# The gated MLP of a hybrid decoder block: convolving the up units where the matmuls left them, in PSUM

## The reference

```python
h = rms_norm(x, g_pre_ffn) * (1.0 + sc2) + sh2
u = h @ w_up                                   # 1024 -> 2 * 2816
u = causal_depthwise_conv(u, conv_w) + conv_b  # width 3, per channel
gate, val = split(u, 2)
y = (gelu(gate) * val) @ w_down                # 2816 -> 1024
x = x + gt2 * rms_norm(y, g_post_ffn)
```

## Time and profile before

| | |
|---|---|
| median of 3 runs | 2221.29 us (2219.47 to 2221.75) |
| the profiled execution | 2221.01 us, of which the span 2218.9 us |
| PE busy | 2169.8 us, 98% of the span |
| DVE, ACT, POOL busy | 1414.3 us (64%), 780.1 us (35%), 313.3 us (14%) |
| mean clock granted to TensorE | 0.995 of full speed |
| ACT copies out of the banks, line 1724 | 176 of 595 ns |
| DVE, lines 2239, 2241, 2242 | 176 each of 646, 955 and 1044 ns on average |

### The profile page before, as it was taken

One profiled execution on the slowest core, in us unless ns is written; L12 is line 12 of the kernel. 1 busy time (PEld: TensorE's weight loads), 2 busy tenths in 40 slices (PEclk: granted clock), 3 DMA queues, 4 the chain that ended last, 5 costly groups with the idle time before them and its releaser, 6 DMA issues.

```text
span 2218.9 us, 32623 instructions
## 1 busy us (share of the span) xinstructions
PE 2169.8 (98%) x12955; PEld 1747.8 (79%) x12955; DVE 1414.3 (64%) x2386; ACT 780.1 (35%) x1537; POOL 313.3 (14%) x182
## 2 busy tenths in 40 slices
PE   6999999999999989999999999999999999999998
PEld 4776788888887768888888778888888877888886
DVE  3577677775866576787565757466565575566654
ACT  3555543334355342222334633211143444211112
POOL 2322354444300013323000000000000000000000
PEclk9999999999999999999999999999999999999999
DMA  9965687787663456767755254666746444666663
GB/s 367 399 239 195 251 292 257 280 303 280 241 257 116 171 190 261 264 259 269 302 200 207 98 209 171 256 257 264 297 158 249 151 147 160 262 247 234 236 244 121
DMA packets 123551, 519.27 MB, mean 234 GB/s; under 512 B 8831, under 2 KB 39817, under 8 KB 74249
## 3 DMA queue, kind: packets, MB, share of 16 engines
q1 hardware_dynamic: 123401, 517.19, 62.8%
HBM read 401.81 MB, written 115.34 MB: 233 GB/s over the span
## 4 chain that ended last, share of the span: by engine, by line
PE 87%; DVE 5%; ACT 3%; issue 2%; DMA 2%; SPq 0%; POOL 0%; DVEq 0%; ACTq 0%; POOLq 0%
PE ps L820 18%; PE ps L822 18%; PE ps L821 18%; PE ps L842 4%; PE ps L844 4%; PE ps L843 4%; PE ps L1279 3%; PE ps L1281 3%; PE ps L1280 3%; PE ps L1255 1%; PE ps L1254 1%; PE ps L1253 1%; PE ps L919 1%; PE ps L966 1%; PE ps L767 1%
## 5 line engine op out<-in xcount | busy, mean ns | idle before, releaser
L820 PE MATMUL ps<-hTh,wt 128*128 128x512 f32 x1416 | 559.7, 395 | 2.2 <-DVE hTl L1876 2.0
L821 PE MATMUL ps<-hTl,wt 128*128 128x512 f32 x1416 | 552.3, 390 | 0.0
L822 PE MATMUL ps<-hTh,wt 128*128 128x512 f32 x1416 | 552.3, 390 | 0.0
L1724 ACT ACTIVATE ub<-ps 128x512 f32<-128x512 f32 x176 | 104.7, 595 | 654.9 <-PE ps L822 642.4
L820 PEld LDWEIGHTS ps<-hTh,wt 128*128 128x128 f32 x1416 | 266.3, 188 | 64.3 <-issue 8.8
L822 PEld LDWEIGHTS ps<-hTh,wt 128*128 128x128 f32 x1416 | 266.4, 188 | 56.2
L821 PEld LDWEIGHTS ps<-hTl,wt 128*128 128x128 f32 x1416 | 266.6, 188 | 53.3
L2239 DVE TENSOR_SCALAR cv<-ub,CW 128x512 f32<-128x512 f32 x176 | 113.7, 646 | 281.6 <-ACT ub L1724 279.3
L721 POOL TENSOR_TENSOR wt<-raw,wt 128x1024 fp32r<-128x1024 f32 x72 | 176.4, 2455 | 318.5 <-ACT wt L1362 311.5
L2242 DVE SCALAR_TENSOR_TENSOR cv<-ub,CW,cv 128x512 f32<-128x512 f32 x176 | 183.8, 1044 | 6.2
L820 PE MATMUL ps<-hTh,wt_more 128*128 128x512 f32 x472 | 186.3, 395 | 0.1
(11 more groups left out here) (350 smaller groups left out, 3492.4 us busy)
## 6 DMA issues: line engine op xcount, KB each, us to landing
wt<-split_w SPq DMA_DIRECT2D x192, 1024.0 KB, 4.9
split_w<-wt SPq DMA_DIRECT2D x92, 1024.0 KB, 7.1
wt_more<-split_w SPq DMA_DIRECT2D x92, 1024.0 KB, 4.9
raw<-in_w_up_dram SPq DMA_DIRECT2D x22, 1024.0 KB, 9.3
XN<-in_w_down_dram SPq DMA_DIRECT2D x32, 512.0 KB, 9.4
XT<-in_w_ada_dram SPq DMA_DIRECT2D x10, 1024.0 KB, 12.0
XN<-in_x_dram SPq DMA_DIRECT2D x4, 2048.0 KB, 11.0
raw<-in_w_in_dram SPq DMA_DIRECT2D x8, 1024.0 KB, 14.9
```

The lines of the kernel that those rows point to most:

```text
L820: mm(ps[:, bank, :], w, hTh[:, k, :], start=(k == 0), stop=False)
L821: mm(ps[:, bank, :], w, hTl[:, k, :], start=False, stop=False)
L822: ins = mm(ps[:, bank, :], wl(slot)[:, k, :], hTh[:, k, :], start=False, stop=(k == KD - 1))
L1724: act.activation(ub[:, u, 2:], ps[:, u, :], ACT.Copy).then_inc(s["acc_taken"], 1)
```

## The change

The copy into `ub` goes. `take_up(u)` reads bank u three times with a scale and a bias: the last tap and the bias for columns 2 to 511, and for columns 0 and 1 the same with a bias that already holds what the two tokens of the last block add. These biases (`EG`) are made by DVE at the start of each block's up stage in six small operations. DVE's `conv(u)` reads the bank for the two other taps, then keeps two columns of it, and only then counts `acc_taken`. The gelu is written back to bank u, the product of gate and value to bank 2 + u (`ps[:, 2 + u]`), and the high and low parts and the four sums are made from there. In blocks 1 to 3, outside the last group, the first half of product 0 goes to `P32` in an operation of its own, and the sums wait for ACT's first copy (`ph_ready`).

PE's waits move with it: units 0 and 1 of a step wait for products 0 and 1 of the step before (`prod_ready`), units 2 and 3 for its last low part (`p_ready`), and the first four tiles of `last_down` for the two products and the last low part of the last step (`first_half`). DVE's wait for the old `conv_done` of a buffer goes, and ACT's `take_up` waits instead for the product of the step before that read the same half of `cv`.

```diff
...
@@ -357,9 +357,10 @@
         Y = fb("Y", [P, TT, D])
-        ub = fb("ub", [P, 4, 2 + BT])
+        EG = fb("EG", [P, 3, 2 * NFF])
+        fb("EG_rest", [P, 4 * (2 + BT) - 6 * NFF])
         cv = fb("cv", [P, 4, BT])
-        P32 = fb("P32", [P, 8, 256])
+        P32 = fb("P32", [P, 5, 256])
         ffn.close()
...
@@ -1192,6 +1195,16 @@
+                def bank_free(at, u):
+                    if at < 4:
+                        pe.wait_ge(s["acc_taken"], eb_ + E_IN)
+                    elif u < 2:
+                        pe.wait_ge(s["prod_ready"], b * (2 * STEPS) + at // 4 * 2 - 1 + u)
+                    else:
+                        pe.wait_ge(s["p_ready"], b * (2 * STEPS) + at // 4 * 2)
@@ -1199,7 +1212,7 @@
                             pe.wait_ge(s["t32_ready"], tb + (4 + u + 1))
-                        pe.wait_ge(s["acc_taken"], eb_ + (E_IN + at - 3))
+                        bank_free(at, u)
                         if f and i == 0 and u >= 2 and not first:
...
@@ -1266,7 +1279,7 @@
                         elif q == 2:
-                            pe.wait_ge(s["acc_taken"], eb_ + (E_IN + 4 * (ST0[f] + 1) + 2 + t + 1))
+                            pe.wait_ge(s["p_ready"], b * (2 * STEPS) + 2 * (ST0[f] + 2))
                         else:
@@ -1290,6 +1303,8 @@
                     late = 1 if first else 0
+                    made = b * (2 * STEPS) + 2 * STEPS
+                    first_half = [("prod_ready", made - 1), ("prod_ready", made), ("p_ready", made), ("p_ready", made)]
                     for u in range(8):
...
@@ -1720,14 +1732,21 @@
                         act.wait_ge(s["unit_done"], ub_ + (n + 1))
-                        act.wait_ge(s["conv_done"], m + (u + 1))
-                        act.activation(ub[:, u, 2:], ps[:, u, :], ACT.Copy).then_inc(s["acc_taken"], 1)
+                        col = 2 * st_ + (u % 2) + NFF * (u // 2)
+                        if jb + u % 2 > 1:
+                            act.wait_ge(s["prod_ready"], jb - 1 + u % 2)
+                        act.wait_ge(s["edges_ready"], b + 1)
+                        for cols, bias in ((slice(2, BT), CW[:, 3, col:col + 1]), (slice(0, 1), EG[:, 0, col:col + 1]),
+                                           (slice(1, 2), EG[:, 1, col:col + 1])):
+                            ins = act.activation(cv[:, u, cols], ps[:, u, cols], ACT.Identity, scale=CW[:, 2, col:col + 1], bias=bias)
+                        ins.then_inc(s["tap_done"], 1)
                         refill(n + RING)
                         sum_high(n + SLOTS)
                     def gelu(u):
-                        act.wait_ge(s["conv_done"], m + (4 + u + 1))
-                        act.activation(cv[:, u, :], cv[:, u, :], ACT.Gelu_apprx_tanh).then_inc(s["gelu_done"], 1)
+                        act.wait_ge(s["conv_done"], m + (u + 1))
+                        act.wait_ge(s["acc_taken"], eb_ + (E_IN + 4 * st_ + u + 1))
+                        act.activation(ps[:, u, :], cv[:, u, :], ACT.Gelu_apprx_tanh).then_inc(s["gelu_done"], 1)
@@ -1745,12 +1764,12 @@
                             act.wait_ge(s["prod_ready"], jb + (u + 1))
-                            act.activation(hidden_at(pTh, 2 * i + u), flat(P32[:, 2 * u:2 * u + 2, :]), ACT.Copy).then_inc(s["ph_ready"], 1)
+                            act.activation(hidden_at(pTh, 2 * i + u), ps[:, 2 + u, :], ACT.Copy).then_inc(s["ph_ready"], 1)
                         return
                     act.wait_ge(s["prod_ready"], jb + 2)
-                    act.activation(flat(pTh[:, i, 0:3, :]), flat(P32[:, 1:4, :]), ACT.Copy).then_inc(s["ph_ready"], 1)
+                    act.activation(flat(pTh[:, i, 0:3, :]), products(256, 1024), ACT.Copy).then_inc(s["ph_ready"], 1)
                     act.wait_ge(s["sums_ready"], (b - 1) * ST0[LG] + (st_ + 1))
-                    act.activation(flat(pTh[:, i, 3:7, :]), flat(P32[:, 4:8, :]), ACT.Copy).then_inc(s["ph_ready"], 1)
+                    act.activation(flat(pTh[:, i, 3:7, :]), flat(P32[:, 0:4, :]), ACT.Copy).then_inc(s["ph_ready"], 1)
...
@@ -2174,6 +2191,15 @@
+                h0, h1 = halo[:, :, 0], halo[:, :, 1]
+                up(tt(EG[:, 0, :], CW[:, 1, :], h1, ALU.mult))
+                up(tt(EG[:, 2, :], CW[:, 0, :], h0, ALU.mult))
+                up(tt(EG[:, 1, :], CW[:, 0, :], h1, ALU.mult))
+                up(tt(EG[:, 0, :], EG[:, 0, :], EG[:, 2, :], ALU.add))
+                up(tt(EG[:, 0, :], EG[:, 0, :], CW[:, 3, :], ALU.add))
+                tt(EG[:, 1, :], EG[:, 1, :], CW[:, 3, :], ALU.add).then_inc(s["edges_ready"], 1)
@@ -2232,25 +2258,26 @@
                         tap = lambda n: CW[:, n, col:col + 1]
-                        edge = halo[:, col, :]
-                        dve.wait_ge(s["conv_done"], m + (u + 1))
-                        up(ts(ub[:, u, 0:2], edge, 1.0, None, ALU.mult))
-                        dve.wait_ge(s["acc_taken"], eb_ + (E_IN + 4 * st_ + u + 1))
-                        up(ts(cv[:, u, :], ub[:, u, 2:], tap(2), tap(3), ALU.mult, ALU.add))
-                        up(ts(edge, ub[:, u, BT:], 1.0, None, ALU.mult))
-                        up(stt(cv[:, u, :], ub[:, u, 1:BT + 1], tap(1), cv[:, u, :], ALU.mult, ALU.add))
-                        stt(cv[:, u, :], ub[:, u, 0:BT], tap(0), cv[:, u, :], ALU.mult, ALU.add)\
-                            .then_inc(s["conv_done"], 1)
+                        dve.wait_ge(s["tap_done"], m + (u + 1))
+                        up(stt(cv[:, u, 1:], ps[:, u, 0:BT - 1], tap(1), cv[:, u, 1:], ALU.mult, ALU.add))
+                        stt(cv[:, u, 2:], ps[:, u, 0:BT - 2], tap(0), cv[:, u, 2:], ALU.mult, ALU.add).then_inc(s["conv_done"], 1)
+                        ts(halo[:, col, :], ps[:, u, BT - 2:], 1.0, None, ALU.mult).then_inc(s["acc_taken"], 1)
                     def gated(u):
                         dve.wait_ge(s["gelu_done"], jb + (u + 1))
-                        dve.wait_ge(s["conv_done"], m + (4 + 2 + u + 1))
-                        tt(P32[:, 2 * u:2 * u + 2, :].rearrange("p a n -> p (a n)"), cv[:, u, :], cv[:, 2 + u, :], ALU.mult)\
+                        dve.wait_ge(s["conv_done"], m + (2 + u + 1))
+                        dve.wait_ge(s["acc_taken"], eb_ + (E_IN + 4 * st_ + 2 + u + 1))
+                        cut = 256 if u == 0 and f < LG and not first else 0
+                        if cut:
+                            up(tt(P32[:, 4, :], ps[:, 0, 0:256], cv[:, 2, 0:256], ALU.mult))
+                        tt(ps[:, 2 + u, cut:], ps[:, u, cut:], cv[:, 2 + u, cut:], ALU.mult)\
                             .then_inc(s["prod_ready"], 1)
                     def token_half_sums():
-                        a21, a11, a22, a12, s1, s2, s3, s4 = (P32[:, j, :] for j in range(8))
+                        a11, a22, a12 = (products(256 * j, 256 * j + 256) for j in range(1, 4))
+                        s1, s2, s3, s4, a21 = (P32[:, j, :] for j in range(5))
                         dve.wait_ge(s["prod_ready"], jb + 2)
+                        dve.wait_ge(s["ph_ready"], jb + 1)
                         up(tt(s1, a21, a22, ALU.add))
@@ -2261,13 +2288,13 @@
                             k = 2 * i + part
-                            tt(hidden_at(pTl, k), flat_(P32[:, 2 * part:2 * part + 2, :]), hidden_at(pTh, k).bitcast(fp32),
+                            tt(hidden_at(pTl, k), ps[:, 2 + part, :], hidden_at(pTh, k).bitcast(fp32),
                                ALU.subtract).then_inc(s["p_ready"], 1)
                             return
                         if part:
                             dve.wait_ge(s["sums_ready"], (b - 1) * ST0[LG] + (st_ + 1))
                         of = slice(3, 7) if part else slice(0, 3)
-                        tt(flat_(pTl[:, i, of, :]), flat_(P32[:, of.start + 1:of.stop + 1, :]),
+                        tt(flat_(pTl[:, i, of, :]), (flat_(P32[:, 0:4, :]) if part else products(256, 1024)),
                            flat_(pTh[:, i, of, :].bitcast(fp32)), ALU.subtract).then_inc(s["p_ready"], 1)
```

More of the change, by code:

```diff
@@ L210 @@
 ACT_STEPS, DVE_STEPS = 28, 76
-UP_STEPS0, UP_STEPS = 16 * STEPS, 19 * ST0[LG] + 16 * NS[LG]
+UP_STEPS0, UP_STEPS = 4 * STEPS + 5, 8 * ST0[LG] + 4 * NS[LG] + 5
 class Steps:
@@ L394, in hymba_block @@
           tok_tr tok_taken dstate_mm state_ready pool_ready pool_mm intra_mm hgo_mm hgo_taken oss_ready or_ready g_softplus g_sub g_exp o_squared o_ready hgt_tr
-          k_copied att_hi att_lo p_norm p_norm_a recip vd_ready p_masked s_mm row_max probs es_ready p_tr p_copied pv_mm tile_done half_ready premul fin_r fin_done conv_done gelu_done
+          k_copied att_hi att_lo p_norm p_norm_a recip vd_ready p_masked s_mm row_max probs es_ready p_tr p_copied pv_mm tile_done half_ready premul fin_r fin_done edges_ready tap_done conv_done gelu_done
           prod_ready sums_ready ph_ready p_ready y_added y_copied dn_tile t_added dq0 dq1 dq2 dq3 act_steps dve_steps dve_up act_ada pool_steps pe_fence dve_fence
@@ L398, in hymba_block @@
```

(15 more changed lines are left out.)

## The result

The changed kernel takes 2239.3 us (median of 4 runs, 2237.9 to 2243.5) against 2221.5 (2219.5 to 2222.4): 17.8 us slower. The estimated ratio of the two is 1.0085 with a 95% interval of 1.0071 to 1.0098 (the two medians alone give 1.0080). The forecast was 2238. The profiled execution took 2240.2 us with a span of 2238.5, 19.6 more than the span of before; its mean granted clock was 0.993.

What follows compares the result with a forecast made beforehand. TensorE, busy without a gap in the up stages, was taken as the bound. Stalls 5.7 + 7.3 + 3.0 + 2.7, clock 3.0, less 4.6 returned, gave 17.1 us: about 2238 us, range 2228 to 2256.

Steps and rivals of the forecast that it cites:

- chain from take-up to product: From the start of ScalarE's take-up through VectorE's taps and kept columns to the product: 3.75 us.
- take-up: ScalarE's reading of a finished bank, one wide and two one-column activations: 1.26 us, 0.66 more than before.
- (a) first step: Block 0, first step: product 0 needs a gelu behind a weight copy waiting for a DMA; 5.7 us stall.
- (b) squares: Blocks 0 to 2, step where ScalarE squares the next block's input: late product stalls PE 3.1, 2.1, 2.1 us.
- (c) `last_down`: Behind each block's last step, tiles of 1.36 us want banks early: 1.0 us three times, 2.7 in the last block.
- clock: Granted clock falls to 0.50 once, after the first-step stall of block 0, costing 3.0 us.
- returned: PE's waits on VectorE's adds into `Y` (2.7) and on `XN` (1.9) both go: 4.6 us back.
- the slack: At ordinary changes of step, time left before PE wants the product: 1.5 us, 1.3 where product 0 is cut.
- An ordinary step adds nothing: Product stands 3.95 us into a unit of 5.44, so PE does not wait at ordinary changes of step.
- 17.1: Forecast net slowdown of the whole kernel in us: stalls and clock loss less the returned waits.
- The three kinds of place: First step behind a DMA (5.7), steps with squares (7.3), `last_down` (3.0 + 2.7): stalls in us.
- the rival that the clock falls at short waits too: Four or five more clock drops of 2.9 us at the 2 to 3 us stalls: 2250 to 2253; chance 0.13.

Runs made afterwards that it cites:

- the first repair: Changed kernel with the weight copies put behind the gelus in block 0's first step alone: 2234.05 us, ratio 1.0055 over the kernel before.
- the one with 40 waits: Changed kernel with three more wide activations into scratch ahead of the take-ups of units 2 and 3: 2313.09 us, ratio 1.0411 over the kernel before.

## Why the prediction was right

| step of the forecast | forecast | measured |
|---|---|---|
| chain from take-up to product | 3.75 | 3.72 (1130.80 to 1134.52) |
| take-up | 1.26, small ones up to 0.38 single | 1.26; 0.346 single |
| (a) first step | 5.7 | 5.9 listed, 6.1 between starts |
| (b) squares | 3.1, 2.1, 2.1 | 3.0, 2.0, 2.0 listed, 7.6 between starts in all |
| (c) `last_down` | 3 x 1.0 + 2.7 | 3 x 1.1 + 2.6 between starts |
| clock | 3.0, once | 1.5 + 1.6 + 1.7, behind three waits |
| returned | 4.6 | 5.6 |
| head of block 1's up stage | 0 | 1.5 less, placed by the clock, not by the change |

*The chain and its threshold* are shown: by the rows of the chain in the last step of block 1,

```profile
1130.80 0.78 ACT L1741 ACTIVATE cv<-ps,CW 128x510 f32<-128x510 f32 x1 [3.69 <-PE ps L825]
1131.47 0.59 ACT L1741 ACTIVATE cv<-ps,EG,CW 128x1 f32<-128x1 f32 x2
...
1132.09 0.75 DVE L2262 SCALAR_TENSOR_TENSOR cv<-ps,CW,cv 128x511 f32<-128x511 f32 x1 [3.01 <-ACT cv L1741]
1132.88 0.75 DVE L2263 SCALAR_TENSOR_TENSOR cv<-ps,CW,cv 128x510 f32<-128x510 f32 x1
1133.54 0.15 DVE L2264 TENSOR_SCALAR halo<-ps 128x2 f32<-128x2 f32 x1
1133.82 0.70 DVE L2273 TENSOR_TENSOR ps<-ps,cv 128x512 f32<-128x512 f32 x1
```

and by the two versions with a longer chain: one below the slack without a new wait, one above it with an excess that meets it to 0.1 us. "An ordinary step adds nothing" held in all 36. The measured taps are 749 ns beside 752 of before: an operation with two tensor operands costs the same from PSUM. For one with a single tensor operand the bank is dearer, 808 against 546 ns. The Trainium skill's "Perfetto Trace Analysis" (Optimizing Scalar/DVE Operations) has about 125 ns of access on PSUM against 60 on SBUF, so 65 more; that fits neither.

*The places* are shown by removing each cause alone, and by their sum: 6.1 + 7.6 + 5.9 + 4.8 - 5.6 - 1.5 = 17.3.

*That the total came within 0.2 us of 17.1 is luck.* The three kinds of place together were 0.9 above the forecast and the clock 1.8 above it; what came back was 1.0 more than forecast, and 1.5 came from a place that the change doesn't touch. The mechanism, the places and the size of each wait were right by their own working; that the rest cancelled was not foreseen.

*The clock* was mis-sized: 4.8 us behind three waits, not 3.0 behind one. The drop behind (a) cost 1.5 us, because its first half fell into the wait (the granted clock was 0.50 from 275.1 us and TensorE started again at 278.93), where TensorE has nothing to lose; I had costed it from the earlier trace rows, where TensorE worked through it. And the rival that the clock falls at short waits too was half true: it fell behind two of the other waits, at 1.6 and 1.7 us each.

*What comes back* was right in its effect and incomplete in its cause. The earlier trace rows list 2.7 us on the adds and 1.9 on `XN`, which are 3.1 and 2.1 between starts (0.4 more of short pauses went too). I attributed the return to the taps. For `XN` the timeline of before agrees: in the last step of block 0 three taps took 2.90, 1.66 and 2.87 us for 0.75 each, the last of them right in front of `XN`:

```profile
571.72 2.87 DVE L2242 SCALAR_TENSOR_TENSOR cv<-ub,CW,cv 128x512 f32<-128x512 f32 x1
```

In front of the late adds it shows others:

```profile
919.37 2.60 DVE L2239 TENSOR_SCALAR cv<-ub,CW 128x512 f32<-128x512 f32 x1
922.00 2.24 DVE L2240 TENSOR_SCALAR halo<-ub 128x2 f32<-128x2 f32 x1
...
925.73 2.47 DVE L2207 TENSOR_TENSOR Y<-Y,ps 128x512 f32<-128x512 f32 x4
```

The scale and bias (usually 0.55) and the copy of two columns (0.17) were held for 4.1 us while GpSimd made two subtractions, 919.29 to 924.22. The change removed the one and moved the other to the bank. That each alone is not enough is what the versions with SBUF taps and with the operation put back show; that both together are was read from these rows and not tried. The 1.5 us at the head of block 1's up stage were not foreseen: the first 120 matmuls there, where TensorE waits for the input's parts and works partly at half clock, took 9.9 us more than 0.227 each before and 8.4 after. But over the other versions of the changed kernel the same figure runs from 7.8 to 10.0 (that one with a longer stretch at half clock), so that the 1.5 are no gain of the change. It goes with the place of the stretch at half clock: that began 15.1 us behind the stage's first matmul before (9.9 lost), 11.7 after (8.4), 10.6 in the version with SBUF taps (7.8) and 14.9 in the first repair (9.9). The earlier it falls, the more of it lies in waits. What sets the moment is open.

## What to carry to other kernels

When a buffer's release moves from its first reader to its last, compare the new chain with the time of the work that runs in between: below that it is free, above it every turn pays, and the places where the rhythm differs (a first step behind a DMA, a long job of the releasing engine, a stage with shorter tiles) pay first. Look for those places in the old trace, since they cost nothing there; here each could be cured by a local change of order or of one buffer, and the whole then gained 0.3% (8 us). Price a wait as its listed time and the clock behind it.

## What the runs showed of the hardware

The clock's fall behind a wait isn't a function of the wait alone. Over the profiled executions here except the one with 40 waits, for the waits inside and right behind the up stages: at waits of 5 us and more it fell each time (7); at 2.5 to 3.8 us in 16 of 20; at 1.9 to 2.1 us in 3 of 9; at 1.6 us and less never. The 3.0 us wait of block 0 had it in the version with the last step in SBUF and not in the changed kernel, whose code is equal up to there. One fall took 1.4 to 1.7 us of full-speed work, and up to 2.9 where the stretch at 0.50 lasted longer. Waits that follow one another closely are another case: at the head of block 1's up stage, where waits of 0.4 to 2.1 us follow one another within some 16 us (the earlier trace rows has the last), it fell in all eleven executions.

An activation of one column with two pointer operands takes 346 ns, nearly half of one of 510 columns (777), and two of them 0.59 together.

Small VectorE operations are held by GpSimd as wide ones are: the first two of the edge operations, on 44 columns, took 2.4 and 2.3 us in block 0, where GpSimd was at work (0.20 in block 1), and ScalarE waited 3.8 us for them in front of the first take-up; TensorE had other work. VectorE's timeline of the changed kernel:

```profile
258.35 2.41 DVE L2196 TENSOR_TENSOR EG<-CW,halo 128x44 f32<-128x44 f32 x1
```
